# VectorE instead of GpSimd writes each norm's row form, inside the stage that follows the norm; the memory input's buffer takes over two uses of `z`

## The chip, the cores and the metric

One Trainium2 chip, one NeuronCore. The metric is the device time of one execution in microseconds; three executions of the kernel before gave 1005.23, 999.93 and 1003.98.

## What is computed

Two transformer blocks in float32 on one sequence of 256 tokens and 1024 features. The first block has a gated causal convolution and an attention of 16 heads side by side, a merge of the two, an output matrix and a residual. The second has two layers, each with attention (12 heads over the sequence, 4 over a memory of 256 rows) and a gated feed-forward network with a short convolution along the tokens. Cut to what matters here:

```python
def rms_norm(x, g):
    y = xf * lax.rsqrt(jnp.mean(xf * xf, axis=-1, keepdims=True) + EPS)
    return (y * g.astype(jnp.float32)).astype(x.dtype)
def layer_norm(x, g, b):
    return ((xf - mu) * lax.rsqrt(var + LN_EPS) * g + b).astype(x.dtype)
# second block, for each of two layers (x enters as the rms_norm of the first block)
        o_mem = memory_attention(qm.reshape(...), mem, w_mem_kv)
        mix = jnp.concatenate([o_main, o_mem], axis=-1) @ w_out
        x = layer_norm(ALPHA * x + mix, ln1_g[layer], ln1_b[layer])
        ffn = conv_ffn(x, ffn_w_in[layer], ffn_conv_w[layer], ffn_conv_b[layer], ffn_w_out[layer])
        x = layer_norm(ALPHA * x + ffn, ln2_g[layer], ln2_b[layer])
```

Each norm's result is needed twice: transposed, as the moving operand of the next products, and by rows ("the row form"), for the residual `ALPHA * x` one stage later.

## The kernel before, in words

**Weights.** All weights come as a stream of 300 blocks of 128 x 1024 float32 (512 KB each), in the order of their use. A ring of three slots holds each block three times: `raw` as loaded, `wh` its high part (ScalarE rounds to the fast format, L417) and `wl`, what is left (VectorE subtracts, L815). Every product is then three matmuls: high by high, high by low, low by high. The loop on SyncE (L255) loads block b as soon as the split of block b - 3 has freed its `raw` (semaphore `split_l`). On ScalarE and VectorE a `refill(i, b)` makes the split of block b + 3 once TensorE has used block b. Both engines have these refills written by hand between their other work, in one fixed order per engine, so an instruction that is late holds all that stand behind it.

**Blocks.** TensorE runs a block as `stationary` (24 matmuls of 256 columns, L1330 to L1332), as `wide` (L1358 to L1360) or as a `row` of an output matrix (12 matmuls of 512 columns, L1378 to L1380). `two_stationary` (L1342 on) is the first pair after a norm, fed k by k. The values of the last layer are made at L1759 to L1761.

**Stages of the stream.** First block: values, 8 pairs of heads, then the merge, a loop of turns with two products and one row of `w_o` each. Then norm n1. Layer 0: keys of the memory, keys and compressed keys, 6 pairs of heads, output rows with the memory's heads between them (`finish`), norm n2, FFN of 22 turns (per turn two products and one row), norm n3. Layer 1: values, 6 pairs (`moba`), `finish`, norm n4, FFN, norm n5 and the output.

**A norm** has the sums on VectorE (L861), squares on ScalarE (L431), the root on GpSimd (L297, L299), `z` on VectorE (L889, L893), transposes on TensorE (L1398), gain and shift on VectorE (`xf`, L833 and L836), high parts on ScalarE (L442), low parts on VectorE for even k (L825) and on GpSimd for odd k (`low_odd`, L322).

**The row form** is made by GpSimd's `tail` right behind `low_odd`: `x_tok = z * gain` (L312) and, but at n1, `+ shift` (L315), on 128 x 1024, for each of two token halves: 2 instructions at n1 and 4 at each of n2, n3 and n4. Then `load_gb` (L303, L305) fetches the next gain and shift. `x_tok` is read next by the sum of the following norm.

**Buffers.** `z` also serves as the second buffer of the probabilities (`prs[1]`, L192) in the heads of layer 0 and as the values of the last layer (`v_all`, L193), so both wait for n1's and n3's row form (L673 on ScalarE, L764 on ScalarE and L1283 on VectorE). `memf`, the memory's rows, is loaded by GpSimd's queue (L352), turned into `memh` by ScalarE in two copies (L550) ahead of the merge loop, and into `meml` by GpSimd in one instruction (L368); nothing reads it afterwards.

**Places where the change lands on VectorE.** In the merge loop the turn is `part_c`, two refills, `part_a`, a refill. In the FFN the turn (`body`) is: taps `t_a` (L1239, L1242, which wait for ScalarE's base, L712), a refill, a refill, the gate `t_c` and `ml` (L1250, L825, with ScalarE's `mh` L722 between them), a refill; TensorE waits for the taps before the next first product and for `ml` before the row. In `moba` the turn is: a refill, the copy of turned probabilities (L1294), scores with bias (L909), `o_low`, a refill, then the probabilities (L1303, L1304, L917), which TensorE turns (L1416) at the end of the next two products. `k_s` is copied by ScalarE (L776) behind a refill.

Of the kernel before, what the change touches and what calls it, by code (L numbers as in the profile page):

```python
# [108 lines left out]
def build_program(nc, a):  # L109
    ctx = ExitStack()  # L110
    with ctx:
# [80 lines left out]
        prs = [pr, z[:, :, :].rearrange("p b (h c) -> p b h c", h=2)]  # L192
        v_all = z  # L193
        sq = pr[:, 0, :, :].rearrange("p h c -> p (h c)")
# [18 lines left out]
        first_norm = {"sum": 1, "mean": 2, "x": 1, "half": 1, "off": 5}  # L213
# [71 lines left out]
        def _(pool):  # L285
# [21 lines left out]
            def tail(nm, shift):  # L307

                pool.wait_ge(gb_in, 16 + 32 * (norms.index(nm) - 1))
                for t in range(NT):  # L310
                    norm_wait(pool, nm, "z", t + 1)
                    last = pool.tensor_tensor(x_tok[:, t, :], z[:, t, :], gb[:, 0, :], ALU.mult)  # L312
                    if shift:
                        chain.link(last)
                        last = pool.tensor_tensor(x_tok[:, t, :], x_tok[:, t, :], gb[:, 1, :], ALU.add)  # L315
                    last.then_inc(S[nm, "x"], 1)

# [43 lines left out]
            def skewed_rows(i):  # L361
# [5 lines left out]
            pool.wait_ge(mem_h, 2)  # L367
            pool.tensor_tensor(meml[:, :, :], memf[:, :, :], memh[:, :, :].bitcast(F32), ALU.subtract  # L368
                               ).then_inc(mem_l, 1)
# [3 lines left out]
            tail("n1", False)  # L373
            norm_wait(pool, "n1", "x", 2)
            load_gb(a["ln1_g_2"][0], a["ln1_b_2"][0])
            for i in range(PAIRS2):
# [10 lines left out]
                for h in range(2):  # L387
                    for t in range(NT):
                        c = 8 + 2 * h + t
                        p = prc[i % 2][:, t, h, 0:NCMP]  # L390
                        pool.tensor_scalar(p, p, rg[:, c:c + 1], None, ALU.mult).then_inc(S["p3", "prob_pool"], 1)

            for nm, g, b, row in (("n2", "ln2_g_2", "ln2_b_2", 0),
# [17 lines left out]
        def _(act):  # L411
# [135 lines left out]
            act.wait_ge(mem_in, 16)  # L547
            for n in range(2):
                part = slice(n * KT // 2, (n + 1) * KT // 2)
                act.activation(memh[:, part, :], memf[:, part, :], ACT.Copy).then_inc(mem_h, 1)  # L550
# [1432 lines left out]
```

## Time and profile before

| | us |
|---|---|
| median of three runs | 1003.98 |
| lowest and highest run | 999.93, 1005.23 |
| the profiled execution, its own time | 1001.48 |
| span of the profiled execution | 999.7 |
| granted TensorE clock over the span, share of full | 0.989 |

A row of the timeline gives the start, the busy time of the merged instructions, the engine, the line, the operation, what it writes and reads, and in brackets how long the engine stood idle before it and who ended that. Engines: PE is TensorE, DVE VectorE, ACT ScalarE, POOL GpSimd, SP SyncE. Instructions of one engine overlap a little: the next one starts before the busy time of the last is over. The granted clock is the share of full speed that TensorE was given.

### The profile page before, as it was taken

To read this page: it belongs to the slowest core of one execution; us is meant where nothing else is said; L and a number is where in the kernel's file an instruction comes from. 1 tells how busy PE (TensorE), PEld (TensorE's weight loads), DVE (VectorE), ACT (ScalarE), POOL (GpSimd) and SP (SyncE) were. 2 spreads that over 40 slices of the span, in tenths; PEclk is the share of its full clock that TensorE was granted. 3 is DMA by queue.
4 is the path that set the end of the run, shared out by engine and by line. 5 is a ranking of instruction groups with operands and counts; after the bars stand their busy time and mean duration, and the time that the engine had idled before them with its cause. 6 is when DMAs were issued, how large, how long until landed. Compare 5 with 4: busy or idle time off the path is not lost.

```text
span 999.7 us, 19995 instructions
## 1 busy us (share of the span) xinstructions
PE 948.9 (95%) x7006; PEld 859.3 (86%) x7006; DVE 664.5 (66%) x1212; ACT 527.0 (53%) x967; POOL 127.9 (13%) x154
## 2 busy tenths in 40 slices
PE   8999999999999888999799999998899989999995
PEld 5899999999899877757699999987788679999995
DVE  5566666666666857965866666678567666666666
ACT  5545555555444648754555555545565455555553
POOL 3000000000100402630600000006100150000001
PEclk9999999999999999999999999999999999999998
DMA  7555555556465375314265555553754346555552
GB/s 256 181 190 178 178 178 182 178 175 226 148 210 188 125 254 158 120 37 148 86 231 190 187 188 189 189 193 108 243 179 152 105 148 205 188 184 189 184 189 77
DMA packets 48226, 172.89 MB, mean 173 GB/s; under 512 B 6031, under 2 KB 6479, under 8 KB 48060
## 3 DMA queue, kind: packets, MB, share of 16 engines
q1 hardware_dynamic: 44732, 159.78, 47.9%
q0 software_dynamic: 3456, 12.61, 4.1%
q8 instruction: 24, 0.39, 0.2%
q14 instruction: 14, 0.11, 0.0%
HBM read 171.29 MB, written 1.07 MB: 172 GB/s over the span
## 4 chain that ended last, share of the span: by engine, by line
PE 77%; DVE 10%; ACT 6%; DMA 4%; issue 2%; POOL 1%; SPq 0%; POOLq 0%; ACTq 0%; DVEq 0%
PE bank L1330 17%; PE bank L1331 17%; PE bank L1332 17%; PE ysum L1378 6%; PE ysum L1380 6%; PE ysum L1379 6%; DVE sb_wl L815 5%; DMA sb_raw<-in_stream 4%; ACT sb_wh L417 2%; PE bank L1409 1%; PE ysum L1416 1%; PE ysum L1423 1%; ACT sb_xh L442 1%; DVE sb_z L861 1%; ACT sb_pr L462 1%
## 5 line engine op out<-in xcount | busy, mean ns | idle before, releaser
L815 DVE TENSOR_TENSOR sb_wl<-sb_raw,sb_wh 128x1024 fp32r<-128x1024 f32 x300 | 388.4, 1297 | 169.2 <-ACT sb_wh L417 168.3
L1330 PE MATMUL bank<-sb_xh,sb_wh 128*128 128x256 f32 x1360 | 383.3, 282 | 3.2 <-DVE sb_t_a L1242 2.5
L1331 PE MATMUL bank<-sb_xl,sb_wh 128*128 128x256 f32 x1360 | 379.8, 279 | 0.0
L1332 PE MATMUL bank<-sb_xh,sb_wl 128*128 128x256 f32 x1360 | 379.8, 279 | 0.0
L417 ACT ACTIVATE sb_wh<-sb_raw 128x1024 fp32r<-128x1024 f32 x300 | 315.0, 1055 | 116.2 <-PE ysum L1380 46.7
L1330 PEld LDWEIGHTS bank<-sb_xh,sb_wh 128*128 128x128 f32 x1360 | 256.3, 188 | 12.6 <-DVE sb_t_a L1242 3.5
L1332 PEld LDWEIGHTS bank<-sb_xh,sb_wl 128*128 128x128 f32 x1360 | 257.9, 190 | 0.0
L1331 PEld LDWEIGHTS bank<-sb_xl,sb_wh 128*128 128x128 f32 x1360 | 255.4, 188 | 1.5
L1378 PE MATMUL ysum<-sb_wh,sb_mh 128*128 128x512 f32 x208 | 81.7, 393 | 3.6 <-DVE sb_ml L825 3.6
L1379 PE MATMUL ysum<-sb_wl,sb_mh 128*128 128x512 f32 x208 | 81.7, 393 | 0.0
L1380 PE MATMUL ysum<-sb_wh,sb_ml 128*128 128x512 f32 x208 | 81.6, 393 | 0.0
L297 POOL TENSOR_SCALAR sb_st<-sb_st 128x1 f32<-128x1 f32 x12 | 4.3, 358 | 492.6 <-ACT sb_pr L431 488.5
L722 ACT ACTIVATE sb_mh<-sb_t_c 128x256 fp32r<-128x256 f32 x44 | 18.4, 419 | 90.4 <-DVE sb_t_c L1250 90.4
L712 ACT ACTIVATE sb_t_a<-bank,sb_convf 128x256 f32<-128x256 f32 x44 | 24.9, 566 | 47.3 <-PE bank L1332 43.0
L1378 PEld LDWEIGHTS ysum<-sb_wh,sb_mh 128*128 128x128 f32 x208 | 39.5, 190 | 10.4 <-issue 3.9
L462 ACT ACTIVATE sb_pr<-sb_sc,sb_mx 128x128 f32<-128x128 f32 x80 | 35.6, 448 | 23.1 <-DVE sb_mx L909 23.1
L1380 PEld LDWEIGHTS ysum<-sb_wh,sb_ml 128*128 128x128 f32 x208 | 39.5, 190 | 8.3
L1379 PEld LDWEIGHTS ysum<-sb_wl,sb_mh 128*128 128x128 f32 x208 | 39.3, 189 | 6.4
L1239 DVE SCALAR_TENSOR_TENSOR sb_t_a<-bank,sb_convf,sb_t_a 128x255 f32<-128x255 f32 x44 | 21.2, 482 | 27.0 <-ACT sb_t_a L712 26.9
L1330 PE MATMUL bank<-sb_mixh,sb_wh 128*128 128x256 f32 x128 | 36.3, 283 | 0.8 <-DVE sb_wl L815 0.8
L825 DVE TENSOR_TENSOR sb_ml<-sb_t_c,sb_mh 128x256 fp32r<-128x256 f32 x44 | 21.2, 481 | 23.9 <-ACT sb_mh L722 23.9
L1331 PE MATMUL bank<-sb_mixl,sb_wh 128*128 128x256 f32 x128 | 36.0, 281 | 0.0
(265 smaller groups left out, 1439.0 us busy)
## 6 DMA issues: line engine op xcount, KB each, us to landing
sb_raw<-in_stream SPq DMA_DIRECT2D x300, 512.0 KB, 3.3
sb_bias<-rel_rows POOLq DMA_DIRECT2D x12, 384.0 KB, 3.8
sb_bias<-in_alibi POOLq DMA_DIRECT2D x8, 256.0 KB, 3.1
sb_gb<-in_ln_g POOLq DMA_DIRECT2D x4, 512.0 KB, 4.1
sb_gb<-in_ln_b POOLq DMA_DIRECT2D x4, 512.0 KB, 6.5
sb_x_tok<-in_x SPq DMA_DIRECT2D x2, 512.0 KB, 3.9
sb_memf<-in_mem_t POOLq DMA_DIRECT2D x1, 1024.0 KB, 6.2
out<-sb_x_tok SPq DMA_DIRECT2D x2, 512.0 KB, 2.6
```

The costliest lines, as they stand in the source:

```text
L417: act.activation(wh[slot][:, :, :], raw[slot][:, :, :], ACT.Copy).then_inc(split_h, 1)
L462: act.activation(to[:, branch, h, cols], src, ACT.Exp, bias=mx[:, c:c + 1], scale=-1.0, accum_out=den[:, c:c + 1]).then_inc(S[ph, "exp"], 1)
L712: act.activation(t_a[:, :], bank[0][:, 0:T], ACT.Identity, bias=convf[:, layer, bass.ds(i, 1), 3], scale=convf[:, layer, bass.ds(i, 1), 2] ...
L815: dve.tensor_tensor(wl[slot][:, :, :], raw[slot][:, :, :], wh[slot][:, :, :].bitcast(F32), ALU.subtract).then_inc(split_l, 1)
L825: dve.tensor_tensor(dst, src, high, ALU.subtract).then_inc(s, 1)
L1239: cf.link(dve.scalar_tensor_tensor(out=t_a[:, 1:T], in0=bank[0][:, 0:T - 1], scalar=convf[:, layer, bass.ds(i, 1), 1], in1=t_a[:, 1:T], op ...
L1330: pe.matmul(out, wh[slot][:, k, :], mov_h(k), start=k == 0, stop=False)
L1331: pe.matmul(out, wh[slot][:, k, :], mov_l(k), start=False, stop=False)
L1332: last = pe.matmul(out, wl[slot][:, k, :], mov_h(k), start=False, stop=k == KT - 1)
L1378: pe.matmul(out, th[:, t * P:(t + 1) * P], hw, start=start, stop=False)
L1379: pe.matmul(out, th[:, t * P:(t + 1) * P], lw, start=False, stop=False)
L1380: last = pe.matmul(out, tl[:, t * P:(t + 1) * P], hw, start=False, stop=stop)
```

## The change

- GpSimd's `tail` goes. VectorE gets the same instructions as `gained` (times gain) and `shifted` (plus shift): for n1 two `gained` in layer 0's `finish`; for n2 and n4 one of `gained`, `shifted`, `gained`, `shifted` at the end of each of the first four turns of the FFN, which are written out ahead of the loop; for n3 the same four in turns 1 to 4 of `moba`, between the second refill and the probabilities.
- GpSimd's `load_gb` moves behind those: after the heads for n1, and for n3 behind the bias loads of the last heads.
- `z` keeps its content until then. `prs[1]` and the values of the last layer lie in `memf`; the waits for n1's and n3's row form in front of them go.
- The memory's halves: ScalarE makes `memh` in two copies at the end of turns 0 and 1 of the merge loop, VectorE makes `meml` in two subtractions at the end of turns 1 and 2; GpSimd's instruction goes. These turns are written out ahead of the loops.

```diff
-        prs = [pr, z[:, :, :].rearrange("p b (h c) -> p b h c", h=2)]
+        prs = [pr, memf[:, :, :].rearrange("p (b h s) t -> p b h (s t)", b=2, h=2)]
         v_all = z
+        v_both = memf[:, :, :].rearrange("p (t s) c -> p t (s c)", t=NT)
...
-            def tail(nm, shift):
-
-                pool.wait_ge(gb_in, 16 + 32 * (norms.index(nm) - 1))
-                for t in range(NT):
-                    norm_wait(pool, nm, "z", t + 1)
-                    last = pool.tensor_tensor(x_tok[:, t, :], z[:, t, :], gb[:, 0, :], ALU.mult)
-                    if shift:
-                        chain.link(last)
-                        last = pool.tensor_tensor(x_tok[:, t, :], x_tok[:, t, :], gb[:, 1, :], ALU.add)
-                    last.then_inc(S[nm, "x"], 1)
...
-            pool.wait_ge(mem_h, 2)
-            pool.tensor_tensor(meml[:, :, :], memf[:, :, :], memh[:, :, :].bitcast(F32), ALU.subtract
-                               ).then_inc(mem_l, 1)
             for t in range(NT):
                 rstd("n1", t, EPS_RMS)
             low_odd("n1")
-            tail("n1", False)
-            norm_wait(pool, "n1", "x", 2)
-            load_gb(a["ln1_g_2"][0], a["ln1_b_2"][0])
...
+            norm_wait(pool, "n1", "x", 2)
+            load_gb(a["ln1_g_2"][0], a["ln1_b_2"][0])
...
                 low_odd(nm)
-                tail(nm, True)
-                norm_wait(pool, nm, "x", 2)
-                load_gb(a[g][row], a[b][row])
                 if nm == "n3":
                     pool.wait_ge(S["p3", "max"], 12 * PAIRS2)
                     for i in range(PAIRS2):
                         relative("p5", i, 4)
+                norm_wait(pool, nm, "x", 2)
+                load_gb(a[g][row], a[b][row])
...
+            for n in range(2):
+                products(n)
+                if n == 0:
+                    act.wait_ge(mem_in, 16)
+                part = slice(n * KT // 2, (n + 1) * KT // 2)
+                act.activation(memh[:, part, :], memf[:, part, :], ACT.Copy).then_inc(mem_h, 1)
...
-            norm_wait(act, "n1", "x", 2)
+            act.wait_ge(mem_l, 2)
...
-            norm_wait(act, "n3", "x", 2)
-            act.activation(v_all[:, 1, 0:512], bank[6][:, :], ACT.Copy).then_inc(v_up[1], 1)
+            act.activation(v_both[:, 1, 0:512], bank[6][:, :], ACT.Copy).then_inc(v_up[1], 1)
...
+            def gained(nm, t):
+
+                dve.wait_ge(gb_in, 16 + 32 * (norms.index(nm) - 1))
+                return dve.tensor_tensor(x_tok[:, t, :], z[:, t, :], gb[:, 0, :], ALU.mult)
+
+            def shifted(nm, t):
+
+                norm_wait(dve, nm, "off", t + 1)
+                dve.tensor_tensor(x_tok[:, t, :], x_tok[:, t, :], gb[:, 1, :], ALU.add).then_inc(S[nm, "x"], 1)
+
+            def tail_step(nm, n):
+
+                if n % 2 == 0:
+                    gained(nm, n // 2).then_inc(S[nm, "off"], 1)
+                else:
+                    shifted(nm, n // 2)
...
+            for n in range(3):
+                products(n)
+                if n:
+                    part = slice((n - 1) * KT // 2, n * KT // 2)
+                    dve.wait_ge(mem_h, n)
+                    low(meml[:, part, :], memf[:, part, :], memh[:, part, :].bitcast(F32), mem_l)
...
                 transposed(1)
+                if ph == "pm3":
+                    gained("n1", 0).then_inc(S["n1", "x"], 1)
                 refill(0, r0 + 5)
                 o_low(ph, 1, PAIRS2 + 1, 2)
+                if ph == "pm3":
+                    gained("n1", 1).then_inc(S["n1", "x"], 1)
                 refill(0, r0 + 6)
...
-                with dve.Fori(0, FT - 2) as i:
+                for n in range(4):
+                    body(n)
+                    tail_step(nm, n)
+                with dve.Fori(4, FT - 2) as i:
                     body(i)
-                body(FT - 2)
-
-            ffn("f0", 0, B_FFN0)
+                body(FT - 2, True)
+
+            ffn("f0", 0, B_FFN0, "n2")
...
-            norm_wait(dve, "n3", "x", 2)
-            dve.tensor_copy(v_all[:, 0, 0:512], bank[5][:, :]).then_inc(v_up[1], 1)
+            dve.tensor_copy(v_both[:, 0, 0:512], bank[5][:, :]).then_inc(v_up[1], 1)
...
                 refill(0, b + 1)
+                if 0 < i < 5:
+                    tail_step("n3", i - 1)
                 dve.wait_ge(S["p5", "exp"], i * 4 + 4)
```

## Rows read from the trace of the kernel before

**Rows 1.** The page: busy time, share of the span and instructions of each engine.

```profile
PE 948.9 (95%) x7006; PEld 859.3 (86%) x7006; DVE 664.5 (66%) x1212; ACT 527.0 (53%) x967; POOL 127.9 (13%) x154
```

**Rows 2.** Whom TensorE waited for, whole span: total us, times, longest.

```profile
PE ysum L1330 <- DVE sb_wl L815: 3.7, 3, 2.2
PE ysum L1378 <- DVE sb_ml L825: 3.6, 2, 2.0
...
PE ysum L1759 <- DVE sb_wl L815: 2.6, 2, 2.3
PE bank L1330 <- DVE sb_t_a L1242: 2.5, 2, 2.0
...
PE bank L1409 <- ACT sb_k_s L776: 2.4, 1, 2.4
...
PE bank L1330 <- DVE sb_wl L815: 1.5, 3, 0.8
...
PE ysum L1358 <- DVE sb_wl L815: 0.6, 2, 0.4
```

**Rows 3.** GpSimd's groups: busy us, mean ns, idle before and releasers.

```profile
L312 POOL TENSOR_TENSOR sb_x_tok<-sb_z,sb_gb 128x1024 f32<-128x1024 f32 x8 | 23.9, 2998 | 0.0
...
L368 POOL TENSOR_TENSOR sb_meml<-sb_memf,sb_memh 128x2048 fp32r<-128x2048 f32 x1 | 4.6, 4615 | 26.4 <-ACT sb_memh L550 26.4
```

**Rows 4.** VectorE's timeline in the merge loop and behind norms n1, n2 and n3.

```profile
268.93 5.93 DVE L815 TENSOR_TENSOR sb_wl<-sb_raw,sb_wh 128x1024 fp32r<-128x1024 f32 x2 [0.90 <-ACT sb_wh L417]
...
341.53 2.97 DVE L815 TENSOR_TENSOR sb_wl<-sb_raw,sb_wh 128x1024 fp32r<-128x1024 f32 x1 [1.04 <-ACT sb_wh L417]
...
494.11 1.68 DVE L825 TENSOR_TENSOR sb_ml<-sb_t_c,sb_mh 128x256 fp32r<-128x256 f32 x1 [0.49 <-ACT sb_mh L722]
...
688.40 14.19 DVE L815 TENSOR_TENSOR sb_wl<-sb_raw,sb_wh 128x1024 fp32r<-128x1024 f32 x5 [0.98 <-ACT sb_wh L417]
```

**Rows 5.** Stretches: PE, PEld, DVE, ACT, POOL busy (instructions), granted clock, DMA share, GB/s.

```profile
284.00:326.00 42.00, 42.00 (x297) 39.39 (x296) 26.72 (x37) 18.21 (x21) 0.00 (x0) 1.00 0.55 186
341.00:350.00 9.00, 6.94 (x46) 6.77 (x46) 8.26 (x15) 5.54 (x9) 6.93 (x5) 0.81 0.35 116
486.00:500.00 14.00, 9.97 (x57) 8.18 (x57) 12.34 (x9) 7.06 (x10) 13.05 (x7) 0.88 0.25 78
```

**Rows 6.** The chain that ended last: two loads behind norms n1 and n3.

```profile
348.78 5.84 DMA sb_raw<-in_stream
...
702.76 8.14 DMA sb_raw<-in_stream
```

**Rows 7.** The page's DMA issues: the stream, median us to landing.

```profile
sb_raw<-in_stream SPq DMA_DIRECT2D x300, 512.0 KB, 3.3
```

**Rows 8.** GpSimd's timeline behind norm n1: the first gain load.

```profile
347.04 0.63 POOL L303 DMA_DIRECT2D sb_gb<-in_ln_g  x1 [0.30 <-POOL sb_x_tok L312]
```

**Rows 9.** VectorE's timeline in a turn of the first FFN, far from the norms.

```profile
607.68 0.48 DVE L1239 SCALAR_TENSOR_TENSOR sb_t_a<-bank,sb_convf,sb_t_a 128x255 f32<-128x255 f32 x1 [0.63 <-ACT sb_t_a L712]
...
610.63 1.23 DVE L815 TENSOR_TENSOR sb_wl<-sb_raw,sb_wh 128x1024 fp32r<-128x1024 f32 x1 [0.71 <-ACT sb_wh L417]
...
616.06 0.48 DVE L1239 SCALAR_TENSOR_TENSOR sb_t_a<-bank,sb_convf,sb_t_a 128x255 f32<-128x255 f32 x1 [0.63 <-ACT sb_t_a L712]
```

**Rows 10.** VectorE's timeline in turn 1 of the last attention.

```profile
725.07 1.23 DVE L815 TENSOR_TENSOR sb_wl<-sb_raw,sb_wh 128x1024 fp32r<-128x1024 f32 x1 [0.53 <-ACT sb_wh L417]
726.22 0.16 DVE L1303 TENSOR_SCALAR sb_deng<-sb_den 128x4 f32<-128x4 f32 x1
...
726.62 1.01 DVE L917 TENSOR_SCALAR sb_pr<-sb_pr,sb_rden 128x128 f32<-128x128 f32 x4
```

**Rows 11.** TensorE's timeline behind it: the turns of the probabilities.

```profile
727.75 0.82 PE L1416 MATMUL ysum<-sb_ident,sb_pr 128*128 128x128 f32 x6
```

**Rows 12.** VectorE's timeline late in layer 0's output rows.

```profile
466.52 1.22 DVE L815 TENSOR_TENSOR sb_wl<-sb_raw,sb_wh 128x1024 fp32r<-128x1024 f32 x1 [1.81 <-ACT sb_wh L417]
...
470.50 1.23 DVE L815 TENSOR_TENSOR sb_wl<-sb_raw,sb_wh 128x1024 fp32r<-128x1024 f32 x1 [2.42 <-ACT sb_wh L417]
```

More of the change, by code:

```diff
@@ L211, in build_program @@
                     "turned": KT, "xf": 6, "xf_act": 2, "xh": KT, "xl_dve": 4, "xl_pool": 4}
-        first_norm = {"sum": 1, "mean": 2, "x": 1, "half": 1, "off": 5}
+        first_norm = {"sum": 1, "mean": 2, "x": 1, "half": 1, "off": 2}
         for what in per_norm:
@@ L545, in _, with products @@
             merge(0)
[L547 to L550, printed above, removed]
-            with act.Fori(0, KT - 2) as i:
+            def products(i):
                 for n in range(3):
@@ L554, in _ @@
                 merge(i + 1)
+            for n in range(2):
[4 more added lines that the diff above has]
+                act.activation(memh[:, part, :], memf[:, part, :], ACT.Copy).then_inc(mem_h, 1)
+            with act.Fori(2, KT - 2) as i:
+                products(i)
             refill(KT - 2, B_MIX + 2)
@@ L1048, in _, with products @@
             refill(0, B_MIX + 1)
-            with dve.Fori(0, KT - 2) as i:
+            def products(i):
                 part_c(i + 1, i * RING + (B_MIX + 3))
@@ L1054, in _ @@
                 refill(i, B_MIX + 4)
+            for n in range(3):
[4 more added lines that the diff above has]
+                    low(meml[:, part, :], memf[:, part, :], memh[:, part, :].bitcast(F32), mem_l)
+            with dve.Fori(3, KT - 2) as i:
+                products(i)
             part_c(KT - 1, B_KM0 - 3)
@@ L1231, in _, with ffn @@
             refill(0, B_KM + 1)
-            def ffn(ph, layer, b0):
+            def ffn(ph, layer, b0, nm):
                 cf = Chain(dve, dchf[layer], 1)
@@ L1257, in ffn, with body @@
                 refill(0, b0 + 1)
-                def body(i):
+                def body(i, last=False):
                     taps(i + 1)
                     refill(i, b0 + 2)
-                    if isinstance(i, int):
+                    if last:
                         gated(i + 1, i * RING + (b0 + 4), 1)
@@ L1282, in _ @@
             dve.wait_ge(used, B_QK)
-            norm_wait(dve, "n3", "x", 2)
-            dve.tensor_copy(v_all[:, 0, 0:512], bank[5][:, :]).then_inc(v_up[1], 1)
-            dve.tensor_copy(v_all[:, :, 512:PAIRS2 * P], bank[7][:, :].rearrange("p (t c) -> p t c", t=NT)
+            dve.tensor_copy(v_both[:, 0, 0:512], bank[5][:, :]).then_inc(v_up[1], 1)
+            dve.tensor_copy(v_both[:, :, 512:PAIRS2 * P], bank[7][:, :].rearrange("p (t c) -> p t c", t=NT)
                             ).then_inc(v_up[1], 1)
@@ L1320, in _ @@
             refill(0, B_FFN1 - 1)
-            ffn("f1", 1, B_FFN1)
+            ffn("f1", 1, B_FFN1, "n4")
             norm_sum("n5", N_BLOCKS - 1, ALPHA, True, "n4")
@@ L1426, in values @@
             def values(i, h):
-                return lambda t: v_all[:, t, i * P + h * DH:i * P + (h + 1) * DH]
+                return lambda t: v_both[:, t, i * P + h * DH:i * P + (h + 1) * DH]
             def warm_up(count, bk=bank[3]):
@@ L1522, in memory_keys @@
                     turn_x(nm, n)
-            pe.wait_ge(mem_l, 1)
+            pe.wait_ge(mem_l, 2)
             memory_keys(B_KM0, "n1")
```

## The prediction

> **What bounds the kernel now.** The busy times come first: TensorE is busy 95% of the span, VectorE 66%, GpSimd 13% [rows 1]. So a shorter kernel must take idle time or slow time from TensorE. The view of who waited for whom names its stalls [rows 2]: 3.7 and 1.5 us behind splits (`wl`, line 815) in front of stationary blocks, 3.6 behind `ml`, 2.6 and 0.6 behind splits in front of the blocks of `v`, 2.5 behind the taps' `t_a`, 2.4 behind `k_s`. Some 17 us, nearly all released by VectorE. Its timeline says why [rows 4]: a split that takes 1.23 us in mid-stage [rows 9] took 2.97 at 341.53, five in a row took 14.19 from 688.40, and the small `ml` at 494.11 took 1.68. In those stretches GpSimd ran its 14 row-form instructions of about 3 us, and its 4.6 us subtraction for the memory input fell on the two splits that took 5.93 from 268.93 [rows 3, 4]. The table of stretches adds the clock [rows 5]: from 341 to 350 TensorE's granted clock averaged 0.81, from 486 to 500 it was 0.88, so part of each ran at 1.2 instead of 2.4 GHz, after waits of about 2 us.
>
> **Part by part: gains.** All sums are made against the profiled execution, 1001.48 us with a span of 999.7; it lies 2.5 us under the median of the three runs, 1003.98.
>
> *Memory halves.* GpSimd's 4.6 us instruction goes; VectorE gets two subtractions of 1024 columns, some 1.2 us each by the split's row [rows 9], one at the end of each of two loop turns, and ScalarE's two copies come apart. The stretch of two splits to 5.93 us cost a stationary block 0.8, the longest wait in its line [rows 2]; bounds 0 and 0.8. The new instructions have cover: VectorE is busy 26.7 of 42 us in these turns [rows 5]. If that cover were gone, 2.4. **0.8 saved.**
>
> *Norm n1.* The split at 341.53 falls from 2.97 to 1.23: 1.75 earlier for everything behind it on VectorE, up to the split that frees the ring's buffer. The chain then goes through a load, not through TensorE [rows 6]: these 512 KB landed after 5.84 us where 3.3 is the median of 300 [rows 7], and GpSimd had issued two gain loads of 512 KB from 347.04 on [rows 8]. Those move to behind n1's row form, past the heads, so I take 4.0 for this load, nearer the median: 1.8 more. The block that waited 2.2 (of the 3.7) starts 3.6 earlier. That TensorE also ran partly at half clock adds nothing here, since split and load set the end. Bounds: 1.75 if the load stays as slow, 4.3 if it takes the median. **3.6 saved.**
>
> *Norm n2.* The wait for the taps was 2.0, the longest of its line; the other, at n4, was 2.5 - 2.0 = 0.5 [rows 2] and I take that here too: 1.5. The wait for `ml` was 2.0; `ml` would take about a quarter of 1.68, 1.25 less, and the split ahead of it was stretched as well, so all 2.0 goes. Clock: 14 us at 0.88 lost 1.7 [rows 5]; it went with the waits and I take it back. **5.2 saved**, bounds 3.0 and 5.5. Late next is the taps' own base, 0.5.
>
> *Norm n3.* Five splits in 14.19 us become five starts 1.15 apart, about 6, so VectorE is 8 us ahead. Of the first wait (2.3, the longest in the 2.6) 1.7 goes, as at n1, and 0.6 stays, because ScalarE gives that `wh` only at the end of the norm; the rest, 0.3 and 0.6, goes. `k_s` waited 2.4 because ScalarE stood in front of a load that landed 8.14 us after its issue at 702.76 [rows 6]; it was issued late, by the last split, and beside two gain loads. With the splits 8 us ahead it is there in time; 0.4 stays. 1.7 + 0.9 + 2.0 = 4.6, and blocks that no longer restart from idle give a little more. **5.0 saved**, bounds 3.5 and 5.6. The copies of `v` no longer wait for the row form; they waited for TensorE anyway: 0.
>
> *Norm n4.* The other `ml` wait, 3.6 - 2.0 = 1.6, and two block starts that make up most of 1.5 - 0.8 = 0.7 [rows 2]. **2.0 saved**, bounds 1.2 and 2.3.
>
> **Costs.** 14 row-form instructions of 1024 columns on VectorE. The nearest row is the split, same form and size: 1.23 us, the next instruction starting 1.15 after it [rows 9, 10]. Those are the bounds; meeting GpSimd it could be 3, but nothing large is left there.
> - n1, two instructions late in the heads' last stage: VectorE stood idle 1.81 us before the split at 466.52 and 2.42 before the one at 470.50 [rows 12]. Each fits: 0; without that cover 1.15 each.
> - n2 and n4, eight, at the end of the first four turns of each FFN, ahead of the taps. A turn has 0.63 us free before the taps and 0.71 before the second split behind them [rows 9], together 1.34 against 1.15. The taps come 0.5 later, but a turn is 8.38 us for three blocks [rows 9] and TensorE needs the taps two blocks (5.6) after their base: 0. If it shows in full, 9.2.
> - n3, four in the attention loop, between the second split and the probabilities. Here is no gap: the split starts at 725.07, the probabilities run from 726.62 to 727.63, TensorE turns them from 727.75 [rows 10, 11]. The first half is ready about 0.6 before that, so the turn comes 1.15 - 0.6 = 0.55 late; the copy of the turned probabilities, behind one more split on VectorE's queue, comes the full 1.15 late. I take 0.85 each, **3.4 lost**, bounds 2.2 and 4.6. Queued behind it are the probabilities, the next split and the copy; TensorE waits for the first and the last.
> - Gain loads now fall into loops: 0, up to 0.5 each. GpSimd's queue waits for the row form ahead of them; behind it stands the next norm's small work, tens of us off: 0. Its bias loads for the last heads pass ahead of the n3 wait: 0. SyncE's queue has only later or earlier splits to wait for, counted above.
>
> Sum: 0.8 + 3.6 + 5.2 + 5.0 + 2.0 - 3.4 = 13.2 saved, 988.3; I say 988.5.
>
> **A rule beside the rows.** The splits are stretched only while GpSimd has large instructions of its own in SBUF [rows 3, 4]; if both merely slowed each other by sharing, I would keep half of the 16.6 gained, near 997. The Trainium skill (SBUF — State Buffer, Who interferes with whom) says that a VectorE instruction with two SBUF inputs contends with a GpSimd one that reads SBUF, under a lock held for a whole instruction. By that rule the whole stretch goes, as in the sum above.
>
> **The rivals.**
> A. *Partial gain, 993 to 999.* The stalls pass from split to load: TensorE arrives earlier and meets loads that need 3.3 to 5 us whatever the splits do. For it: two pieces of the chain are loads [rows 6]. Against it: both were slow beside gain loads, and issued late by splits. Half the gains, 8.3, less 3.4: 996.6.
> B. *The attention loop hides the row form too.* Something else than VectorE sets that loop; cost 0.5, gains at their upper bounds, 18.4: 983.6.
> C. *Slower: VectorE's queue becomes the bound.* Each row form delays taps, splits and, through the buffer's release, the next load. It decides where the free time around it is under 1.15 us: 0.6 in the attention loop, 1.34 in the FFN, a margin of 0.2. If it fails everywhere, 14 times 1.15 is 16.1, and the gains are at their lower bounds, 0 + 1.75 + 3.0 + 3.5 + 1.2 = 9.5, since the same queue holds them: 1001.5 - 9.5 + 16.1 = 1008. Against: 66% busy, and both gaps of the FFN's turn repeat. The Trainium skill (Perfetto Trace Analysis, Optimizing Scalar/DVE Operations) says that work may be moved off a saturated VectorE, even to GpSimd, which is the opposite of this change; it adds that the two share a port.
> D. *Nothing to tell from before.* The waits stay, only the two slow loads shorten (1.8 + 2.0), and the attention loop pays 3.4: 1001.
>
> **Numbers.** Forecast 0.57, A 0.22, B 0.08, D 0.07, C 0.06. The forecast's own bounds are 985.3 (18.4 less 2.2) and 996.6 (9.5 less 4.6). The range goes to 983.5 for B and to 997 for the middle of A; what it leaves out is part of A, C and D. A measurement of this kernel can tell about 0.5% (5 us) from no change. Faster by more: the forecast, B and most of A, 0.87; within it D and the edge of A, 0.08; slower C, 0.05.
>
> **What would show it.** GpSimd's groups of 1024 columns gone, its busy time down by some 45 us; VectorE with 16 more instructions of 1.2 but hardly more busy time, as no split is over 1.3; TensorE's waits for `wl` and `ml` at the norms under 1 us; the granted clock at 1.0 around 341 and 486; the load at n1 near 4 us; the wait for `k_s` under 0.5; in four turns of the attention loop a new wait of 0.5 to 1.2 for the probabilities or their copy; none in the FFN loops. Waits behind the taps in the FFNs' first turns would show C; waits that stay, with loads in front of them, A.

## The result and the profile after the change

The changed kernel takes 988.64 us, median of four runs (988.37 to 989.58), against 1002.36 for four runs of the kernel before (999.93 to 1005.23): a ratio of 0.9854 as recorded, 95% interval 0.9832 to 0.9876 (the two medians alone give 0.9863). Three executions stand apart and are in no comparison: one of experiment 1 took 1880.53 us, and the kernel before, executed again beside the experiments, once took 2279.85 and once 1175.07 (at a granted clock of 0.753) where it otherwise took 999.93 to 1005.23. The profiled execution took 988.38 with a span of 986.7 us at a mean granted clock of 0.994; before it was 1001.48, 999.7 and 0.989. So 13.0 us of span are to be found. Each kernel has its own line numbers: L804 here is the split that was L815 before, and it has another number in some experiments.

The page's busy times and the costliest VectorE group, against [rows 1]:

```profile
PE 944.5 (96%) x6998; PEld 857.1 (87%) x7006; DVE 658.9 (67%) x1228; ACT 526.1 (53%) x967; POOL 83.0 (8%) x139
...
L804 DVE TENSOR_TENSOR sb_wl<-sb_raw,sb_wh 128x1024 fp32r<-128x1024 f32 x300 | 366.5, 1223 | 166.0 <-ACT sb_wh L402 165.0
```

GpSimd lost 44.9 us of busy time. VectorE took over 16 instructions of about 1.22 us, 19.5 us in all, and is still 5.6 us less busy, because no split takes longer than the others any more. Their new groups, from the table of groups (busy us, mean ns):

```profile
L891 DVE TENSOR_TENSOR sb_x_tok<-sb_z,sb_gb 128x1024 f32<-128x1024 f32 x8 | 9.7, 1217 | 0.0
L896 DVE TENSOR_TENSOR sb_x_tok<-sb_x_tok,sb_gb 128x1024 f32<-128x1024 f32 x6 | 7.3, 1218 | 0.0
...
L814 DVE TENSOR_TENSOR sb_meml<-sb_memf,sb_memh 128x1024 fp32r<-128x1024 f32 x2 | 2.4, 1218 | 0.0
```

Whom TensorE waited for (total us, times, longest), against [rows 2]:

```profile
PE ysum L1353 <- DVE sb_wl L804: 2.8, 3, 1.2
...
PE ysum L1439 <- DVE sb_pr L923: 1.8, 5, 0.5
...
PE bank L1381 <- DVE sb_wl L804: 1.4, 2, 1.1
...
PE bank L1353 <- DVE sb_t_a L1261: 0.9, 2, 0.5
...
PE ysum L1401 <- DVE sb_ml L814: 0.9, 2, 0.5
...
PE bank L1432 <- ACT sb_k_s L765: 0.6, 1, 0.6
PE ysum L1782 <- DVE sb_wl L804: 0.5, 1, 0.5
```

The splits' wait in front of the values is down from 2.6 to 0.5, `ml` from 3.6 to 0.9, the taps from 2.5 to 0.9, `k_s` from 2.4 to 0.6. New is the wait for the probabilities `pr`, five times for 1.8 (before: once, 0.2): four of the five, 1.6 us, are in the attention loop, and experiment 1 shows what else is paid there. The first line, waits for splits of 2.8 in all, is at the compressed keys behind n1; experiments 6 to 8 come back to it.

The same stretches as [rows 5], for the changed kernel (PE, PEld, DVE, ACT, POOL busy, granted clock, DMA share, GB/s):

```profile
284.00:326.00 42.00, 42.00 (x296) 39.35 (x295) 28.92 (x39) 18.56 (x21) 0.00 (x0) 1.00 0.54 182
341.00:350.00 9.00, 7.63 (x64) 7.18 (x63) 8.22 (x18) 5.22 (x9) 0.00 (x0) 1.00 0.40 127
486.00:500.00 14.00, 13.36 (x93) 12.40 (x94) 9.99 (x14) 8.86 (x13) 0.00 (x0) 1.00 0.60 193
```

VectorE's timeline behind n1 and n3, against [rows 4]:

```profile
341.26 1.23 DVE L804 TENSOR_TENSOR sb_wl<-sb_raw,sb_wh 128x1024 fp32r<-128x1024 f32 x1 [1.04 <-ACT sb_wh L402]
...
680.44 3.50 DVE L804 TENSOR_TENSOR sb_wl<-sb_raw,sb_wh 128x1024 fp32r<-128x1024 f32 x3 [0.98 <-ACT sb_wh L402]
```

Both traces cut at the same instructions of TensorE show where the 13.0 us went. The last two columns are experiments 3 and 4, told below. Times are from the start of the first instruction of a part to that of the next, in TensorE's timeline.

| stretch (us) | before | after | no row form | on GpSimd, same places |
|---|---|---|---|---|
| start to merge loop | 257.9 | 259.2 | | |
| merge loop to n1's transposes | 73.05 | 71.58 | 71.58 | 71.58 |
| n1's first pair to compressed keys | 15.23 | 13.13 | 13.14 | 13.03 |
| to the first heads' scores | 33.51 | 32.84 | 32.61 | 33.34 |
| n2's first pair to FFN 0's first row | 13.99 | 10.86 | 10.89 | 10.88 |
| that row to its fifth | 35.23 | 33.58 | 33.57 | 33.59 |
| n3's transposes to the first scores | 34.82 | 29.45 | 29.47 | 29.45 |
| attention loop, first turn with row form | 7.97 | 9.09 | 7.96 | 10.13 |
| next three turns | 24.59 | 27.53 | 24.55 | 30.48 |
| n4's first pair to FFN 1's first row | 14.14 | 11.06 | 11.32 | 10.89 |
| that row to its second | 8.82 | 8.45 | 8.47 | 8.46 |
| second to fifth | 25.62 | 25.13 | 25.12 | 25.12 |

Saved: 1.5 in the merge loop, 2.8 behind n1, 4.8 behind n2, 5.4 behind n3, 3.9 behind n4. Lost: 4.1 in the attention loop, 0.2 in front of n4's first pair and 1.2 before the merge loop, which the change doesn't touch. Sum 12.9; the rest lies in parts that differ by hundredths. Two of these terms carry something that is not the change's. Of the 1.5, 0.2 lies in the four warm-up matmuls ahead of the loop's first product (0.46 us instead of 0.67, behind a wait of 0.9 instead of 0.7): the start had given it away, and five of the experiments have 71.8 instead of 71.58 here with the memory's halves unchanged. And the start differs by the clock: from 10 to 20 us the granted clock was 0.83 in the changed kernel's execution and 1.00 in the other. Of the twelve profiled executions of this document, six had 0.83 there and took 258.6 to 259.7 us to the merge loop, and six had 1.00 and took 257.6 to 258.6.

### The profile page after: what moved, and what is told of

Same layout as the page of the kernel before. It is cut to its first block, busy times and chain, and to the rows that moved or that the text cites. A ratio compares the mean times of both kernels' runs of the same rounds, so it can differ in the third digit from the quotient of the medians.

```text
span 986.7 us, 19868 instructions
## 1 busy us (share of the span) xinstructions
PE 944.5 (96%) x6998; PEld 857.1 (87%) x7006; DVE 658.9 (67%) x1228; ACT 526.1 (53%) x967; POOL 83.0 (8%) x139
## 4 chain that ended last, share of the span: by engine, by line
PE 81%; DVE 7%; ACT 6%; DMA 3%; issue 2%; POOL 1%; SPq 0%; POOLq 0%; DVEq 0%; ACTq 0%
PE bank L1353 17%; PE bank L1354 17%; PE bank L1355 17%; PE ysum L1401 7%; PE ysum L1403 7%; PE ysum L1402 7%; DMA sb_raw<-in_stream 2%; ACT sb_wh L402 2%; DVE sb_wl L804 2%; PE bank L1432 2%; PE ysum L1439 1%; ACT sb_pr L447 1%; PE ysum L1446 1%; DVE sb_sc L915 1%; DVE sb_z L850 1%
## 5 line engine op out<-in xcount | busy, mean ns | idle before, releaser
L804 DVE TENSOR_TENSOR sb_wl<-sb_raw,sb_wh 128x1024 fp32r<-128x1024 f32 x300 | 366.5, 1223 | 166.0 <-ACT sb_wh L402 165.0
L1355 PE MATMUL bank<-sb_mixh,sb_wl 128*128 128x256 f32 x128 | 36.0, 281 | 0.0
L814 DVE TENSOR_TENSOR sb_ml<-sb_t_c,sb_mh 128x256 fp32r<-128x256 f32 x44 | 18.7, 425 | 24.2 <-ACT sb_mh L712 24.2
```

The source lines that it names most:

```text
L804: dve.tensor_tensor(wl[slot][:, :, :], raw[slot][:, :, :], wh[slot][:, :, :].bitcast(F32), ALU.subtract).then_inc(split_l, 1)
L814: dve.tensor_tensor(dst, src, high, ALU.subtract).then_inc(s, 1)
L1355: last = pe.matmul(out, wl[slot][:, k, :], mov_h(k), start=False, stop=k == KT - 1)
```

## Experiments

All are edits of the changed kernel. Ratios are the recorded ones to the kernel before; an experiment without a ratio was executed once, and its total can't be told from another to 3 us (experiment 2), so its stretches are read.

**1. The row form in another gap of the attention's turn.** In the changed kernel's trace VectorE stands idle 1.65 us between the scores and `mixl`:

```profile
710.79 0.42 DVE L814 TENSOR_TENSOR sb_mixl<-ysum,sb_mixh 128x256 fp32r<-128x256 f32 x1 [1.65 <-ACT sb_mixh L574]
711.74 1.23 DVE L804 TENSOR_TENSOR sb_wl<-sb_raw,sb_wh 128x1024 fp32r<-128x1024 f32 x1 [0.52 <-ACT sb_wh L402]
712.88 1.22 DVE L891 TENSOR_TENSOR sb_x_tok<-sb_z,sb_gb 128x1024 f32<-128x1024 f32 x1
...
714.43 1.01 DVE L923 TENSOR_SCALAR sb_pr<-sb_pr,sb_rden 128x128 f32<-128x128 f32 x4
```

```diff
                     score_min("p5", 0, h, bank[3 + h], NO_KEY)
+                if 0 < i < 5:
+                    tail_step("n3", i - 1)
                 if i:
...
                 refill(0, b + 1)
-                if 0 < i < 5:
-                    tail_step("n3", i - 1)
```

> The changed kernel with one move: in the last attention's turns the row form of n3 stands ahead of the low part of the output (behind the scores), where VectorE stood idle 1.65 us in every turn, and not ahead of the probabilities. My theory (the four instructions of 1.15 us cost what they cost, 4.1 us by the two traces, only because VectorE has no free time in front of the probabilities): the turns go back from 9.16 us to about 8.15, the waits for the probabilities vanish, 984.5 us, ratio to the kernel before 0.982. Rival (the loop is longer because of the work on VectorE or a buffer in memf, wherever it stands): still 9.1 us a turn, 988.6.

Measured: 983.56 us, median of five runs (982.79 to 987.98), ratio 0.9824 (0.9801 to 0.9847); the profiled one took 983.02 with a span of 981.4. The loop's turns are back at 7.99 and 24.56. In its timeline the row form sits in the old gap and 0.51 of it is left:

```profile
707.71 1.22 DVE L891 TENSOR_TENSOR sb_x_tok<-sb_z,sb_gb 128x1024 f32<-128x1024 f32 x1
709.44 0.42 DVE L814 TENSOR_TENSOR sb_mixl<-ysum,sb_mixh 128x256 fp32r<-128x256 f32 x1 [0.51 <-ACT sb_mixh L574]
...
711.94 1.01 DVE L923 TENSOR_SCALAR sb_pr<-sb_pr,sb_rden 128x128 f32<-128x128 f32 x4
```

TensorE's timeline tells the loss apart, first in the changed kernel, then here, at the turns of the probabilities and the product with the values:

```profile
715.03 1.01 PE L1439 MATMUL ysum<-sb_ident,sb_pr 128*128 128x128 f32 x6 [0.46 <-DVE sb_pr L923]
...
717.14 0.66 PE L1446 MATMUL ysum<-sb_pt,sb_memf 128*64 128x256 f32 x4 [0.24 <-issue]
```

```profile
713.08 0.82 PE L1439 MATMUL ysum<-sb_ident,sb_pr 128*128 128x128 f32 x6
...
714.69 0.66 PE L1446 MATMUL ysum<-sb_pt,sb_memf 128*64 128x256 f32 x4
```

VectorE's copy of the turned probabilities, for which the product waits, in the changed kernel and here:

```profile
716.49 0.55 DVE L1315 COPY sb_pt<-ysum 128x384 f32<-128x384 f32 x1
```

```profile
714.00 0.55 DVE L1315 COPY sb_pt<-ysum 128x384 f32<-128x384 f32 x1
```

Of the 1.0 us that a row form costs, 0.46 is the wait for `pr`; from the turns to the product it is 2.11 instead of 1.61 us. Of these 0.50, 0.19 is the turns, which take 1.01 instead of 0.82 when they start behind a wait, and 0.31 is the late copy: it ends at 717.04, and the product starts at 717.14. The loss was a matter of place, not of load on VectorE. This version has the lowest median found and, by its stretches, all that the loop had lost.

**2. The changed kernel again**, beside the first.

> The changed kernel, again, beside the others: 988.6 us. Second sample of the half-clock phases: if they are set by the change, one of 3.4 us lies at n4 and one in the first block; if they fall by chance, the one in the first block is gone or elsewhere and n4 has 3.4 or 6.8.

Measured: 989.15, ratio 0.9862 (0.9843 to 0.9882). Its profiled span was 989.5 where the first was 986.7, with the same instructions in the same order. Of what the expectation set against each other, neither came out whole: the low clock in the first block was there again (0.83 from 10 to 20 us), the one at n4 was gone (1.00 from 784 to 791 where the first execution had 0.76), and a new one lay elsewhere. The heads of layer 0 took 62.28 us instead of 59.17; from 396 to 406 us the granted clock was 0.66 (PE, PEld, DVE, ACT, POOL busy, clock, DMA share, GB/s), where the first execution had 1.00:

```profile
396.00:406.00 10.00, 8.53 (x49) 6.54 (x50) 8.20 (x46) 5.86 (x22) 5.79 (x9) 0.66 0.45 140
```

A mean of 0.66 over 10 us is 6.8 us at 1.2 GHz, 0.34 of 10 being half of that. So a single execution can't tell 3 us. Stretches can, if the granted clock inside them is read too.

**3. No row form at all.** The 14 instructions are left out and only their semaphores are counted up: `x_tok` keeps old values, so the residuals and the output leave out the gain and shift of the norms.

```diff
-                return dve.tensor_tensor(x_tok[:, t, :], z[:, t, :], gb[:, 0, :], ALU.mult)
+                return dve
...
-                dve.tensor_tensor(x_tok[:, t, :], x_tok[:, t, :], gb[:, 1, :], ALU.add).then_inc(S[nm, "x"], 1)
+                dve.sem_inc(S[nm, "x"], 1)
```

> The changed kernel without the row form's 14 instructions (x_tok is not updated after the norms, only the semaphores move; the residual is not computed rightly). My theory: ten of the fourteen are free where they stand, so only the attention's 4.1 us goes: 984.5 us, and every FFN turn, norm and output row stays within 0.1 us. Rival (VectorE's queue is near its bound, each instruction costs some tenths): 980 or below.

Measured: 985.66, ratio 0.9825 (0.9804 to 0.9846); column 4 of the table. The turns of the loop (7.96, 24.55) are those of experiment 1 (7.99, 24.56), so nothing is left to gain there. Its median lies above experiment 1's 983.56, and its profiled execution has heads of 60.52 us where the changed kernel's has 59.17, at a granted clock of 0.83 from 395 to 405. The FFN and the other norms stay within 0.1 as expected; n4's first stretch is 0.26 longer (11.32, as in experiment 1) at a granted clock of 0.57 from 784 to 788. The ten instructions at n1, n2 and n4 cost nothing; the four at n3 cost 1.0 each where the change puts them.

**4. GpSimd in the same places.** VectorE only signals where it would write the row form, and GpSimd writes it.

```diff
             def tail_step(nm, n):
-                if n % 2 == 0:
-                    gained(nm, n // 2).then_inc(S[nm, "off"], 1)
-                else:
-                    shifted(nm, n // 2)
+                dve.sem_inc(go, 1)
...
+                    for n in range(4):
+                        step(nm, n, True)
```

> The changed kernel with the 14 instructions at the same places in time but on GpSimd, which VectorE's queue asks for each. Theory 1, mine: the stretch of VectorE's splits to about 3.4 us comes back at each of them, but in mid-stage turns there is slack for most of it: no loss in the FFN or under 0.5 us per instruction, about 1 to 2.5 us per instruction in the attention loop: 986 to 996 us. Theory 2 (it is the engine that matters; beside GpSimd VectorE loses as much anywhere as behind a norm): as slow as the kernel before, 998 or more. Theory 3 (only the place in time matters): 988 or less.

Measured: 992.57, ratio 0.9889 (0.9869 to 0.9908). In the FFN turns it costs nothing (33.59); in the attention loop it costs 8.1 us against no row form, twice what VectorE's own instruction costs. The timelines of GpSimd and of VectorE in the first such turn (DVEq is VectorE's sequencer, which signals):

```profile
713.02 3.33 POOL L322 TENSOR_TENSOR sb_x_tok<-sb_z,sb_gb 128x1024 f32<-128x1024 f32 x1 [1.70 <-DVEq L914]
```

```profile
712.89 1.23 DVE L828 TENSOR_TENSOR sb_wl<-sb_raw,sb_wh 128x1024 fp32r<-128x1024 f32 x1 [0.53 <-ACT sb_wh L426]
714.04 2.35 DVE L1337 TENSOR_SCALAR sb_deng<-sb_den 128x4 f32<-128x4 f32 x1
...
716.63 1.01 DVE L934 TENSOR_SCALAR sb_pr<-sb_pr,sb_rden 128x128 f32<-128x128 f32 x4
```

The split had begun first and kept its 1.23; the next instruction, on four columns, took 2.35 where it takes 0.16 [rows 10], and ended at 716.39, with GpSimd's at 716.35. VectorE did not run slower beside GpSimd: it stood until GpSimd's instruction was over. The other three turns show the same (2.34 each, ending 0.03 behind GpSimd's). Not every instruction stands. In a turn of the FFN, beside a GpSimd instruction of 3.38 us from 498.67, the taps, which read one of their tensors from a bank and not from SBUF, kept their 0.48, and only the split behind them was held:

```profile
500.28 0.48 DVE L1269 SCALAR_TENSOR_TENSOR sb_t_a<-bank,sb_convf,sb_t_a 128x255 f32<-128x255 f32 x1 [0.50 <-ACT sb_t_a L726]
...
501.23 1.91 DVE L828 TENSOR_TENSOR sb_wl<-sb_raw,sb_wh 128x1024 fp32r<-128x1024 f32 x1
```

**5. The memory's low half back on GpSimd**, both copies ahead of the loop, as before.

```diff
+            pool.wait_ge(mem_h, 2)
+            pool.tensor_tensor(meml[:, :, :], memf[:, :, :], memh[:, :, :].bitcast(F32), ALU.subtract
+                               ).then_inc(mem_l, 2)
```

> The changed kernel with the memory's halves made as before: both copies on ScalarE ahead of the merge loop, one subtraction of 2048 columns on GpSimd. Theory (this part gave 0.8 to 1.25 us by itself): a wait for a split of about 0.8 us comes back in the merge loop, two splits take 5.9 us, and from n1 on everything is about 1.2 us later. Rival (the part was worth nothing, the difference lay in the stretch before): the start of n1 does not move against the changed kernel.

Measured: 988.56. The merge loop takes 73.14, 1.56 more than in the changed kernel and 1.3 more than the 71.8 of the five experiments whose warm-up matmuls took 0.67 as here; that is the 1.2 expected. Two splits take 6.01 again; TensorE waits 0.9 for one:

```profile
268.60 6.01 DVE L805 TENSOR_TENSOR sb_wl<-sb_raw,sb_wh 128x1024 fp32r<-128x1024 f32 x2 [0.90 <-ACT sb_wh L405]
```

The whole was not longer than the changed kernel's 988.38, since its start took 257.61 at a granted clock of 1.00, 1.5 us less than the changed kernel's 259.15 at 0.83; the stretch shows what the total doesn't.

**6. Two loads beside the stream, early.** GpSimd fetches 2 x 512 KB into the memory's old buffer right behind `low_odd` of n1, 6.6 us earlier than the gain loads came before.

```diff
+            for n, row in enumerate((a["ln1_g_2"][0], a["ln1_b_2"][0])):
+                pool.dma_start(memf[:, 4 * n:4 * n + 4, :].rearrange("p s t -> p (s t)"),
+                               row.partition_broadcast(P)).then_inc(extra_in, 16)
```

> The changed kernel with two more loads of 512 KB of the gains' form on GpSimd's queue behind n1's low parts, where the gain loads stood before (into memf, which holds nothing there; nothing else changes). Theory: the gain loads were part of n1's stall: the stream's load issued at 346.8 lands after 5 us or more in place of 3.4, the pair block behind it starts 1 to 2 us later. What is left of that at the end of the compressed keys (382 us) is what moving them gave there: 0.5 to 1.5 us. Rival (only the split counted): block start and end of stage unmoved.

Measured: 988.27. The stream's load issued at 342.30 took 5.91 us. The chain that ended last has it, then two splits, and TensorE waits 1.20 us at the first pair block among the compressed keys, where it didn't wait in the changed kernel:

```profile
353.43 0.38 PE L1359 MATMUL ysum<-sb_xh,sb_wh 128*128 128x256 f32 x1 [1.20 <-DVE sb_wl L810]
```

Yet both stretches behind n1 are unmoved (13.15, 32.87), as the rival had it: what TensorE lost there it had again before the first heads. This experiment issues the loads earlier than the kernel before did; the next two put them in the old place.

**7 and 8. Norm n1 taken apart.** First only the two row-form instructions go back to GpSimd, behind `low_odd`; then the gain loads too.

```diff
             low_odd("n1")
+            pool.wait_ge(gb_in, 16)
+            for t in range(NT):
+                norm_wait(pool, "n1", "z", t + 1)
+                pool.tensor_tensor(x_tok[:, t, :], z[:, t, :], gb[:, 0, :], ALU.mult
+                                   ).then_inc(S["n1", "x"], 1)
+            norm_wait(pool, "n1", "x", 2)
+            load_gb(a["ln1_g_2"][0], a["ln1_b_2"][0])
```

(The last two lines stand in the second alone.)

> The changed kernel with only n1's two row-form instructions back on GpSimd, right behind low_odd; the gain loads stay behind the heads, where the change has them. Main theory (the row form stretches the splits, the loads are separate): the split behind n1 is back near 3 us, and the stretch from n1's first stationary pair to the first block of the compressed keys is 2.1 us longer, 15.2 for 13.1; the stretch behind it, up to the first heads, stays within 0.3 of 32.8, because the 5.8 us load of the kernel before was slow beside the gain loads, which are absent. Rival (the slow load came from the late split alone, so the gain loads never mattered): that load is again over 5.5 us and the stretch up to the first heads is 33.3 or more.

> As the run above, and with the two gain loads at their old place too, right behind the two row-form instructions on GpSimd. Main theory (the prediction's step for n1: 1.8 us of its 3.6 came from the load beside the gain loads): the load of the stream issued beside them lands after 5.5 us or more, and the stretches up to the first heads together are at least 0.5 us longer than in the run above. Rival (the gain loads cost nothing): the same stretches as in the run above within 0.3 us.

Measured: 989.0 and 990.89. The row form alone makes the first stretch 14.87 (1.74 more; 2.1 were expected) and leaves the second at 32.79: the split takes 2.97 again. With the loads the second is 34.44, 1.65 longer. The chain has the load, and TensorE waits for the split behind it:

```profile
348.13 5.95 DMA sb_raw<-in_stream
```

```profile
356.53 0.58 PE L1354 MATMUL ysum<-sb_xh,sb_wh 128*128 128x256 f32 x1 [2.76 <-DVE sb_wl L809]
```

In the kernel before it was the load of 5.84 and this wait:

```profile
357.08 0.39 PE L1330 MATMUL ysum<-sb_xh,sb_wh 128*128 128x256 f32 x1 [2.19 <-DVE sb_wl L815]
```

So the gain loads did make the pair block late. But experiment 7, without them, waits further on in the same stretch, for splits behind loads of 4.8 and 4.2 us that have no gain load beside them:

```profile
365.24 0.29 PE L1571 MATMUL bank<-sb_wh,sb_blkh 128*16 128x256 f32 x1 [1.11 <-DVE sb_wl L809]
...
372.06 0.29 PE L1571 MATMUL bank<-sb_wh,sb_blkh 128*16 128x256 f32 x1 [1.01 <-DVE sb_wl L809]
```

A block that comes earlier meets these waits, and most of the gain is lost again: at the first heads the kernel before, at a clock of 1.00 from 350 to 360, is only 0.72 behind experiment 7 (33.51 against 32.79). Experiment 8 is 1.65 behind it, with a granted clock of 0.83 there, so up to 0.9 of that came with the clock. The 0.7 is not clear of the spread: executions without gain loads in this stretch took from 32.47 to 33.56 for it (experiments 1 and 10). What is clear is the wait of 2.2 to 2.8 and that little of it reaches the end of the stage.

**9. Eight more instructions in the FFN's turns.** Each of the eight row-form instructions gets a twin that writes to a buffer nobody reads.

```diff
                     body(n)
+                    dve.wait_ge(gb_in, 16 + 32 * (norms.index(nm) - 1))
+                    dve.tensor_tensor(memf[:, 0:4, :].rearrange("p s t -> p (s t)"), z[:, 0, :],
+                                      gb[:, 0, :], ALU.mult)
                     tail_step(nm, n)
```

> The changed kernel with a second instruction of 1024 columns on VectorE beside each of the eight row-form instructions of the two FFNs (it writes memf, which holds nothing then). My reading (free time 0.63 and 0.71 us ahead of and behind the taps, then 0.4 and 0.5 more, and TensorE needs the taps only two blocks on): still nothing lost, the first four turns stay 8.37 us. Rival C of the prediction (the margin is 0.2 us): each of the eight costs about 1 us, 8 us in all.

Measured: 997.03, span 995.3. The FFN stretches are longer by 0.61, 2.23, 0.47 and 0.76: 4.1 for eight, neither the expected 0 nor the rival's 8. The largest piece lies behind the four turns, where the split that was late frees the slot for a load that then runs beside the gain loads, issued at 532.54 and 533.15:

```profile
534.57 7.47 DMA sb_raw<-in_stream
```

More than the rest of the 8.6 us of span, 5.3, lies between the compressed keys and the end of layer 0's heads, which the edit doesn't touch; the granted clock was 0.93 from 360 to 385 and 0.71 from 395 to 405. A mean of 0.93 over 25 and of 0.71 over 10 us is 9.3 us at 1.2 GHz, or 4.7 lost, so most of the 5.3 is clock. In the FFN's turns one instruction is free, the second isn't.

**10. Norm n4's row form back on GpSimd.** The four instructions as before, behind `low_odd`, for n4 alone.

```diff
+                if nm == "n4":
+                    tail(nm)
...
                     body(n)
-                    tail_step(nm, n)
+                    if nm != "n4":
+                        tail_step(nm, n)
```

> The changed kernel with n4's four row-form instructions back on GpSimd right behind n4's low parts. Theory: this gives back what the part is worth without the clock: the ml wait of 1.6 us and the small waits behind it, 1.7 to 2.2 us in all from the transposes of n4 to turn 3 of the FFN. Rival (the shorter half-clock phase at n4, 1.9 us, is also owed to it): 3.7 us, with a phase of 6.8 us.

Measured: 992.18, span 990.4. The three stretches behind n4 grow by 0.6, 1.05 and 1.7: 3.4 us, at a full granted clock. The expectation had 1.7 to 2.2 without a phase at the lower clock and 3.7 with one; it is the larger figure, but without the phase. Besides the waits for `wl` (2.0) and `ml` (1.3), later splits take 3.4 (GpSimd's and VectorE's timelines):

```profile
797.46 3.24 POOL L316 TENSOR_TENSOR sb_x_tok<-sb_x_tok,sb_gb 128x1024 f32<-128x1024 f32 x1
800.65 2.58 POOL L313 TENSOR_TENSOR sb_x_tok<-sb_z,sb_gb 128x1024 f32<-128x1024 f32 x1
803.32 3.25 POOL L316 TENSOR_TENSOR sb_x_tok<-sb_x_tok,sb_gb 128x1024 f32<-128x1024 f32 x1
```

```profile
799.74 1.25 DVE L827 TENSOR_TENSOR sb_ml<-sb_t_c,sb_mh 128x256 fp32r<-128x256 f32 x1 [0.76 <-ACT sb_mh L725]
800.91 3.42 DVE L817 TENSOR_TENSOR sb_wl<-sb_raw,sb_wh 128x1024 fp32r<-128x1024 f32 x1
```

The first split of 3.42 ends at 804.33. GpSimd's second instruction is over at 803.23, 1.1 before: a split waits for its turn and then takes its own 1.2.

## Why the prediction was right, step by step

The mechanism was right. That the predicted 988.5 and the measured 988.64 agree to 0.1 us is luck: the steps are off by up to 1.9 us each, with opposite signs.

- **What bounds the kernel.** Right: the gain came from waits of TensorE that VectorE released. Experiments 5, 7 and 10 bring these waits back by returning instructions to GpSimd alone, at the memory's halves, n1 and n4. For n2 and n3 no experiment did so; there the stretches and the splits' times carry it.
- **The rule beside the rows.** Half of the gains would have meant 997. The whole stretch went: the 300 splits average 1.22. Experiment 4 shows the mechanism directly, and so agrees with what the Trainium skill states (SBUF — State Buffer, Who interferes with whom): the engine that comes second stands for the whole instruction of the first. The page of that title names VectorE instructions with two SBUF inputs and some one-input forms; the one held here for 2.35 us reads one operand of four columns.
- **Memory halves**, predicted 0.8 with bounds 0 and 0.8: measured 1.3, by experiment 5 and by the 1.5 of the table less the 0.2 that the start had given away. The term was undersized: the step took only the wait named for a split (0.8), but the two products in which it lies took 6.81 us instead of 5.65 and the row behind them 2.81 instead of 2.72.
- **Norm n1**, predicted 3.6 as 1.75 for the split and 1.8 for the load. The split is right: 1.74 in experiment 7. For the load the step named the right block and then stopped there. From n1's first pair to the block that had waited 2.2, the kernel before took 20.37 us and the changed one 16.12, 4.3 earlier where 3.6 was predicted. Of that, 2.8 was left at the first heads, because the blocks behind it wait for loads in every version, as experiments 7 and 8 show. So the load gave about 0.7 at the end of the stage, not 1.8. That TensorE's low clock adds nothing, as the step said, is nearly so: the pair of blocks from 344.6 on, in which the clock was down, took 7.30 us before and 6.94 in the changed kernel and in experiment 7.
- **Norm n2**, predicted 5.2: 4.8. Stretch 486 to 500 has a clock of 1.00 now. How the 4.8 divides between waits and clock was not separated, so the 1.7 taken for the clock is neither shown nor refuted.
- **Norm n3**, predicted 5.0: 5.4. `k_s` waits 0.6 instead of the 0.4 taken. The first wait left 0.5, the step said 0.6.
- **Norm n4**, predicted 2.0 with an upper bound of 2.3: 3.9 less the 0.2 in front of it. This is the largest miss. The step added up what was left of the lines of TensorE's waits, and took no term for the clock, which the step for n2 had. In this stretch TensorE of the kernel before ran at a granted clock of 0.66, below [rows 5]'s for n2; in experiment 10, with the same instructions on GpSimd, it was 1.00:

```profile
794.00:804.00 10.00, 8.46 (x45) 7.86 (x46) 7.37 (x13) 4.93 (x12) 5.28 (x7) 0.66 0.01 2
```

```profile
795.00:805.00 10.00, 7.99 (x50) 6.22 (x49) 8.42 (x9) 5.98 (x8) 9.84 (x4) 1.00 0.32 105
```

From n4's first pair to the FFN's first row the kernel before took 14.14 us and experiment 10 took 11.68; over the next four rows it was the other way, 34.4 against 36.3. So the kernel before paid 2.5 us at the low clock and then waited less: matmuls at half the clock fill time that would otherwise be a wait. Experiment 10 has 3.4 with waits of 3.3 in all and no clock loss, so adding up waits works where the clock is full. That the clock is why the waits looked small is argued from these rows; no run held it fixed.
- **Attention loop**, predicted a loss of 3.4 (0.85 each): 4.1, or 1.0 each. Right in place and kind: the new wait for `pr` and a later copy. The step took the mean of a late turn (0.55) and a late copy (1.15); the rows of experiment 1 give 0.46 for the wait, 0.31 for the copy and 0.19 for slower turns behind the wait, a piece the step didn't have.
- **FFN turns, `finish`, gain loads in loops**, predicted 0: 0, by experiment 3. Experiment 9 shows how thin the cover was: a second instruction costs 0.5 on average. The rival that VectorE's queue becomes the bound had its point of decision at the right place, between one and two instructions a turn, but beyond what the change asks.
- **The first 258 us** were 1.2 longer, a term no step could have: they hold no edit, and twelve executions took from 257.6 to 259.7 for them, the upper half at the lower clock from 10 to 20 us. A fifth of a microsecond of it comes back ahead of the merge loop's first product.

- **The rivals.** A (stalls pass from split to load) is what happened at n1: 4.3 us gained at one block, 2.8 left at the first heads. Elsewhere the gains reached the end of their stages. B needed the attention loop to hide the row form: it doesn't where the change puts it, and does in experiment 1's place. C did not come: VectorE's queue held up TensorE in the attention loop alone. D fell with the waits. The bounds of B add up to 18.5, not to the 18.4 used, which changes nothing.

By measured stretches the sum is 1.5 + 2.8 + 4.8 + 5.4 + 3.7 - 4.1 - 1.2 = 12.9 against 13.2 predicted. With the 0.2 put to the start, undersized gains (0.5 for the memory, 0.4 for n3, 1.7 for n4) made up for oversized ones (0.8 at n1, 0.4 at n2), the dearer loop (0.7) and the start (1.0).

## What to carry to other kernels

Large GpSimd instructions on SBUF are not free work beside a VectorE that others wait for: ask which VectorE instruction is next when one starts, since even a tiny one may stand until it ends (0.16 us became 2.35), while another keeps its time (the taps' 0.48). When work is moved onto the critical engine, look in the trace for the gap in its turn: the same four instructions cost 4.1 us in one place and nothing some 4 us earlier in the turn. A sum of waits is a fair price only where the granted clock is full: read both for the stretch. An earlier block is a gain only if the blocks behind it don't wait for something else. And compare stretches between the same instructions, not totals, when a term is below 3 us.

## What the runs showed that was not expected

- A 4-column VectorE instruction took 2.35 us instead of 0.16, because a GpSimd instruction was in progress (experiment 4). A GpSimd instruction of 1024 columns took 2.4 to 2.6 us or 3.0 to 3.4; each of the longer ones in the kernel before and in experiments 4, 7, 8 and 10 began while a split was under way (713.02 beside 712.89 in experiment 4, 797.46 beside a split from 796.75 to 798.46 in experiment 10).
- Two executions of the same kernel differ by 2.8 us of span, the second with 7 us at 1.2 GHz in heads that ran at full clock in the first. What sets such a phase off was not found.
- A load of 512 KB beside two others took 5.9 us in both places tried. Issued at 342 it made TensorE wait 1.2 us, issued at 348 some 2.2 to 2.8; at the end of the stage nothing was left of the first and 0.7, or 1.7 with a lower clock, of the second. Its duration tells neither.
